# mLSTM passes of a two-block kernel: a fourth query buffer, another bank for the turn, another order of the squares, and the query scaling on VectorE

## What is computed

```
m_t   = maximum(b + m, max(dmat))
a     = exp(b + m - m_t)
qk    = einsum(q, k) * exp(dmat - m_t)
num   = a * einsum(q, C) + einsum(qk, v)
den   = a * einsum(q, n) + sum(qk)
h     = num / maximum(abs(den), exp(-m_t))
h_lat = hl_f + flip(hl_b)
y     = sigmoid(o) * rms_norm(h, g) * silu(z)
```

## Time and profile before

| | us |
|---|---|
| median of 3 runs (lowest, highest) | 3209.8 (3208.81, 3211.93) |
| the profiled execution's own time | 3207.7 |
| its span, first to last instruction | 3206.0 |
| TensorE matmul busy in the span | 3024.7 (94%) |
| VectorE busy | 1479.2 (46%) |
| ScalarE busy | 1156.3 (36%) |
| GpSimd busy | 146.7 (5%) |
| mlstm stage of layer 0, from its first score to its last post | 79.2 |
| mlstm stage of layer 1 | 53.9 |

### The profile page before, as it was taken

One profiled execution on the slowest core, in us unless ns is written; L12 is line 12 of the kernel. 1 busy time (PEld: TensorE's weight loads), 2 busy tenths in 40 slices (PEclk: granted clock), 3 DMA queues, 4 the chain that ended last, 5 costly groups with the idle time before them and its releaser, 6 DMA issues.

```text
span 3206.0 us, 38631 instructions
## 1 busy us (share of the span) xinstructions
PE 3024.7 (94%) x15614; PEld 2460.2 (77%) x15614; DVE 1479.2 (46%) x1970; ACT 1156.3 (36%) x1822; POOL 146.7 (5%) x206
## 2 busy tenths in 40 slices
PE   7999999999999999988999699999999899889988
PEld 5777888777788877867888588868877688768666
DVE  4645445544555555383432522153445644432344
ACT  4334233434443343163241521162222534331342
POOL 1000000000000000000000300100000000300100
PEclk9999999999999999999999799999999999989999
DMA  4243232330422221101112311312111022221322
GB/s 172 93 152 110 105 118 88 122 130 27 145 92 95 102 79 58 55 7 61 41 60 76 69 66 47 105 30 72 53 61 58 23 79 86 79 85 53 113 69 79
DMA packets 44710, 257.76 MB, mean 80 GB/s; under 512 B 6344, under 2 KB 6352, under 8 KB 20768
## 3 DMA queue, kind: packets, MB, share of 16 engines
q1 hardware_dynamic: 30528, 204.30, 17.9%
q0 software_dynamic: 14048, 51.56, 5.1%
HBM read 251.56 MB, written 4.28 MB: 80 GB/s over the span
## 4 chain that ended last, share of the span: by engine, by line
PE 85%; DVE 7%; ACT 3%; DMA 2%; issue 2%; POOL 1%; SPq 0%; DVEq 0%; ACTq 0%; POOLq 0%
PE PS L732 14%; PE PS L733 14%; PE PS L734 14%; PE PS L713 7%; PE PS L712 7%; PE PS L714 7%; PE PS L678 2%; PE PS L676 2%; PE PS L677 2%; DVE SMALL L2307 1%; PE PS L913 1%; PE PS L1007 1%; PE PS L1023 1%; PE PS L997 1%; PE PS L992 1%
## 5 line engine op out<-in xcount | busy, mean ns | idle before, releaser
L732 PE MATMUL PS<-HHX,WHX 128*128 128x512 f32 (+1 forms) x1600 | 567.4, 355 | 40.3 <-DVE WLM L2157 31.3
L733 PE MATMUL PS<-HL,WHX 128*128 128x512 f32 (+1 forms) x1600 | 567.7, 355 | 0.0
L1481 ACT ACTIVATE WHX<-W 128x2048 fp32r<-128x2048 f32 x108 | 186.1, 1723 | 611.2 <-DMA W<-in_w 389.5
L732 PEld LDWEIGHTS PS<-HHX,WHX 128*128 128x128 f32 x1600 | 308.2, 193 | 85.7 <-issue 33.2
L734 PE MATMUL PS<-HHX,WLX 128*128 128x512 f32 (+1 forms) x1024 | 355.9, 348 | 0.0
L733 PEld LDWEIGHTS PS<-HL,WHX 128*128 128x128 f32 x1600 | 306.9, 192 | 41.6
L2157 DVE TENSOR_TENSOR WLX<-W,WHX 128x2048 fp32r<-128x2048 f32 x60 | 137.5, 2292 | 381.1 <-ACT WHX L1481 381.0
L713 PE MATMUL PS<-HL,WH 128*128 128x512 f32 x672 | 265.4, 395 | 0.0
L712 PE MATMUL PS<-HH,WH 128*128 128x512 f32 x672 | 263.3, 392 | 0.0
L714 PE MATMUL PS<-HH,WL 128*128 128x512 f32 x672 | 261.7, 389 | 0.0
L2157 DVE TENSOR_TENSOR WL<-W,WH 128x2048 fp32r<-128x2048 f32 x68 | 155.9, 2292 | 221.6 <-ACT WH L1481 221.6
(11 more groups left out here) (500 smaller groups left out, 5711.3 us busy)
## 6 DMA issues: line engine op xcount, KB each, us to landing
W<-in_w SPq DMA_DIRECT2D x172, 1024.0 KB, 4.7
XC<-in_wm POOLq DMA_DIRECT2D x12, 1024.0 KB, 5.1
H<-in_wm POOLq DMA_DIRECT2D x12, 1024.0 KB, 5.7
W<-in_wb SPq DMA_DIRECT2D x24, 512.0 KB, 3.2
W<-in_w SPq DMA_DIRECT2D x8, 768.0 KB, 4.1
ARENA<-mrow POOLq DMA_DIRECT2D x18, 256.0 KB, 4.9
PR<-in_nbias POOLq DMA_DIRECT2D x12, 256.0 KB, 2.9
ARENA<-in_nbias POOLq DMA_DIRECT2D x12, 256.0 KB, 2.9
```

Source lines behind the costliest of these rows:

```text
L732: pe.matmul(dst, wh[:, s, c], hi[:, k, t0:t1], start=k == 0, stop=False)
L733: pe.matmul(dst, wh[:, s, c], lo[:, k, t0:t1], start=False, stop=False)
L1481: act.activation(dst[:, s, 0:n], W[:, s, 0:n], ACT.Copy).then_inc(wh_ready[s], 1)
```

## The change

Six edits, all in the mlstm stage.

1. QS has four buffers, not three; the fourth takes the place that CS0 had, and all eight states CS lie in the enlarged SELP. The fetch of query weights for pass p+4 stands beside the fetch of decays for p+4.
2. The query multiplication leaves GpSimd (`pool_queries` is gone) and is done by VectorE (`dve_queries`): for pass 0 ahead of everything in the stage, for pass p+1 behind `probs` of p+1 and ahead of `dens` of p.
3. The turn of head u writes to bank (u + 1) % 2, a bank of scores. It waits no longer for divide_forward; the forward outputs wait no longer for ml_y; the scores of pair u (u of 3 or more) wait for ml_y of pair u-3.
4. ScalarE takes the squares of the head before ahead of divide_forward, not behind it.
5. The context's decay rows are fetched once (256 values), not twice, and the mask's addition writes the second copy that a masked block needs.
6. ml_u0 and ml_u1 are one semaphore, ml_u, counted to the same places.

```
-    DM, QS = [RST[:, 0:T], DM1, DM2, DM3], [PR[:, 0:T], QS1, QS2]
-    CS = [CS0] + [SELP[:, k * (P + 1):(k + 1) * (P + 1)] for k in range(7)]
+    DM, QS = [RST[:, 0:T], DM1, DM2, DM3], [PR[:, 0:T], QS1, QS2, QS3]
+    CS = [SELP[:, k * (P + 1):(k + 1) * (P + 1)] for k in range(8)]
...
                 pe.wait_ge(sem("ml_zm"), past("ml_zm", ly) + 2 * (u - 1))
+            if u >= 3:
+                pe.wait_ge(sem("ml_y"), past("ml_y", ly) + u - 2)
...
-            if d == 0 and u >= 2:
-                pe.wait_ge(sem("ml_y"), past("ml_y", ly) + u - 1)
...
             pe.wait_ge(sem("ml_scaled"), past("ml_scaled", ly) + u + 1)
-            pe.wait_ge(sem("ml_divf"), past("ml_divf", ly) + min(u + 2, np_ // 2))
...
-                mm = pe.transpose(PS[:, 2, i * P:(i + 1) * P], HB[:, h, T * g + i * P:T * g + (i + 1) * P], IDENT[:, :])
+                mm = pe.transpose(PS[:, (u + 1) % 2, i * P:(i + 1) * P], HB[:, h, T * g + i * P:T * g + (i + 1) * P], IDENT[:, :])
...
             if it["d"] == 0:
-                divide_forward(it)
                 if it["u"]:
                     squares(passes[p - 1])
+                divide_forward(it)
...
+    def dve_queries(dve, st, it):
+
+        ly, l, h = st.layer, it["l"], it["h"]
+        if it["g"]:
+            return
+        done = 16 * state_uses[l % 4] if ly else 0
+        dve.wait_ge(sem(f"ml_bw{l % 4}"), done + 16 * (l // 4 + 1))
+        dve.tensor_tensor(QS[l % 4], QS[l % 4], Q[:, h, 0:T], ALU.mult).then_inc(sem("ml_qs"), 1)
...
+        dve_queries(dve, st, passes[0])
         states(passes[0])
         probs(passes[0])
...
                 probs(passes[p + 1])
+                dve_queries(dve, st, passes[p + 1])
             dens(it)
...
-            src = mrow[ly, row, T:TA].unsqueeze(0).broadcast_to([2, TC]).partition_broadcast(P)
-            dst = DM[p % 4].rearrange("p (a b) -> p a b", a=2)
+            src, dst = mrow[ly, row, T:TA].partition_broadcast(P), DM[p % 4][:, it["d"] * TC:(it["d"] + 1) * TC]
...
                 pool_mask(pool, st, passes[p + 2])
-                pool_queries(pool, st, passes[p + 2])
             if p + 4 < np_:
                 pool_decay_rows(pool, st, passes[p + 4])
-            if p + 3 < np_:
-                pool_query_rows(pool, st, passes[p + 3])
+                pool_query_rows(pool, st, passes[p + 4])
```

More of the change, by code:

```diff
@@ L436, in build @@
     cv = Carve(scratch)
-    DM1, DM2, DM3, QS1, QS2 = (cv(T) for _ in range(5))
-    KTX, CS0 = cv(8, P), cv(P + 1)
+    DM1, DM2, DM3, QS1, QS2, QS3 = (cv(T) for _ in range(6))
+    KTX = cv(8, P)
     assert cv.at <= hyb_at + 2 * KT * SLAB
-    DM, QS = [RST[:, 0:T], DM1, DM2, DM3], [PR[:, 0:T], QS1, QS2]
-    CS = [CS0] + [SELP[:, k * (P + 1):(k + 1) * (P + 1)] for k in range(7)]
+    DM, QS = [RST[:, 0:T], DM1, DM2, DM3], [PR[:, 0:T], QS1, QS2, QS3]
+    CS = [SELP[:, k * (P + 1):(k + 1) * (P + 1)] for k in range(8)]
     HB = K
@@ L452, in build @@
     slot_uses = [len(range(k, n_ml, 4)) for k in range(4)]
-    state_uses = [len(range(k, n_lat, 3)) for k in range(3)]
+    state_uses = [len(range(k, n_lat, 4)) for k in range(4)]
     in_layer0 = dict(
         da_probs=n_da, da_evac=n_da, da_o=n_da, da_max=n_da, da_half=16, da_scaled=8, da_turned=8, da_rs=8, da_y=8,
-        ml_s=n_mu, ml_u0=n_lat, ml_u1=n_lat, ml_c0=n_lat, ml_c=3 * n_lat, ml_masked=n_ml, ml_qs=n_lat, decay=n_ml,
+        ml_s=n_mu, ml_u=2 * n_lat, ml_c0=n_lat, ml_c=3 * n_lat, ml_masked=n_ml, ml_qs=n_lat, decay=n_ml,
         ml_zm=n_ml, ml_o=n_ml, ml_dens=n_mu, ml_divf=n_mu, ml_divb=n_mu, ml_rs=n_mu, ml_scaled=n_mu,
@@ L460, in build @@
         rope_done=8, na_probs=2 * n_na, na_max=n_na, na_values=n_na, v_stored=16 * 8, v_blocks=16 * 7,
-        **{f"ml_bm{k}": 16 * slot_uses[k] for k in range(4)}, **{f"ml_bw{k}": 16 * state_uses[k] for k in range(3)})
+        **{f"ml_bm{k}": 16 * slot_uses[k] for k in range(4)}, **{f"ml_bw{k}": 16 * state_uses[k] for k in range(4)})
     def past(name, layer):
@@ L1148, in states @@
             s0, s1, s2, _ = later_blocks(d)
-            for b, done, groups in ((6, "ml_u0", ((4, 5), (s0,))), (7, "ml_u1", ((s1,), (s2,)))):
+            for b, groups in ((6, ((4, 5), (s0,))), (7, ((s1,), (s2,)))):
                 if l:
@@ L1158, in states @@
                                        skip_group_check=True)
-                mm.then_inc(sem(done), 1)
+                mm.then_inc(sem("ml_u"), 1)
         def ahead(it):
@@ L1188, in outs @@
                     mm = pe.matmul(PS[:, pair + j // 2, (P + 1) * (j % 2):(P + 1) * (j % 2 + 1)],
-                                   QS[l % 3][:, j * P:(j + 1) * P], CS[(4 * l + n) % 8], start=False, stop=True,
+                                   QS[l % 4][:, j * P:(j + 1) * P], CS[(4 * l + n) % 8], start=False, stop=True,
                                    skip_group_check=True)
@@ L2701, in pool_query_rows @@
             return
-        if l >= 3:
-            old = [e["p"] for e in st.passes if e["g"] == 0][l - 3]
+        if l >= 4:
+            old = [e["p"] for e in st.passes if e["g"] == 0][l - 4]
             pool.wait_ge(sem("ml_o"), past("ml_o", ly) + old + 1)
-        pool.dma_start(QS[l % 3], wrow[ly, row, :].partition_broadcast(P)).then_inc(sem(f"ml_bw{l % 3}"), 16)
+        pool.dma_start(QS[l % 4], wrow[ly, row, :].partition_broadcast(P)).then_inc(sem(f"ml_bw{l % 4}"), 16)
     def pool_mask(pool, st, it):
@@ L2712, in pool_mask @@
         v = DM[p % 4].rearrange("p (a b) -> p a b", b=P)
+        src = v
         if it["g"]:
-            v = v[:, 0:4:3, :]
-        n = v.shape[1]
-        mask = (MFWD, MBWD)[d].unsqueeze(1).broadcast_to([P, n, P])
-        pool.tensor_tensor(v, v, mask, ALU.add).then_inc(sem("ml_masked"), 1)
-    def pool_queries(pool, st, it):
-        ly, l, h = st.layer, it["l"], it["h"]
-        if it["g"]:
-            return
-        done = 16 * state_uses[l % 3] if ly else 0
-        pool.wait_ge(sem(f"ml_bw{l % 3}"), done + 16 * (l // 3 + 1))
-        pool.tensor_tensor(QS[l % 3], QS[l % 3], Q[:, h, 0:T], ALU.mult).then_inc(sem("ml_qs"), 1)
+            src, v = v[:, 2 * d:2 * d + 2, :], v[:, 0:4:3, :]
+        mask = (MFWD, MBWD)[d].unsqueeze(1).broadcast_to([P, v.shape[1], P])
+        pool.tensor_tensor(v, src, mask, ALU.add).then_inc(sem("ml_masked"), 1)
     def pool_mlstm(pool, st):
@@ L2735, in pool_mlstm @@
             pool_decay_rows(pool, st, passes[p])
-            if p < 3:
-                pool_query_rows(pool, st, passes[p])
+            pool_query_rows(pool, st, passes[p])
         pool_mask(pool, st, passes[1])
-        pool_queries(pool, st, passes[1])
         for it in passes:
@@ L2843, in _ @@
                 pool_mask(pool, next_st, next_st.passes[0])
-                pool_queries(pool, next_st, next_st.passes[0])
             if st.kind == "mlstm":
```

10 lines of the change are left out of this document (5 added, 5 removed).

## The result

| | before | changed |
|---|---|---|
| device time, median | 3209.3 us (4 runs, 3208.0 to 3211.9) | 3183.1 us (4 runs, 3181.8 to 3184.7) |
| ratio | | 0.9918, 95% interval 0.9900 to 0.9935 |
| profiled execution: own time, span | 3207.7, 3206.0 us | 3184.2, 3182.3 us |
| layer 0 stage, first score to last post | 79.2 us | 62.2 us |
| layer 1 stage | 53.9 us | 44.8 us |

The change saves 26.2 us, 0.8% of the kernel. In the profiled executions the two stages got shorter by 17.0 and 9.1 us, 26.1 together, while the spans differ by 23.7: the changed execution came into the stage of layer 0 2.6 us later (first scores at 1758.40 against 1755.79), and the delay is older than the parts that the change touches, since GpSimd's store of the decay rows ahead of them stands at 1602.89 against 1600.33 already. Between and behind the stages the two executions agree within 0.3 us.

The account below looks back on a forecast made before the run. It held the mlstm stages bound by engines waiting on each other; 15.9 us less in layer 0 and 8.8 in layer 1 made 3207.7 into 3183.0, and the median's 2.1 on top gave 3185 us, range 3174 to 3199.

Parts of the forecast that it names:

- a circle of waits over root, scale, turn and post: Both mlstm stages: engines wait on each other in a loop, none full; cutting it saves 24.7 us together.
- The sum by stages: Pair and end times summed per mlstm stage: layer 0 15.9 us less, layer 1 8.8, together 24.7.
- the context's 5.3 a pair: Layer 0's three context pairs: 5.3 us each instead of 7.1, bounds 3.9 and 7.1, 5.4 us less.
- The one ahead of the stage puts 0.6 us on the path: Start of each stage: VectorE's query multiplication for the first pass adds 0.6 us.
- VectorE and TensorE are nearly equal, they hand work to each other, so 9.0: Latent pairs: VectorE 7.7 + 0.7 us, TensorE 8.1; a pair taken at 9.0, bounds 8.1 and 10.1.
- The port, 0.7 us a pair: Latent pairs: VectorE operations meeting GpSimd masks lose up to 0.73 us each, 0.7 a pair, bounds 0 and 2.2.
- Rival A: Latent pairs: each query multiplication and scale meets a GpSimd mask, pairs take 10.1 us; 3195 us, chance 0.17.
- Squares first: ScalarE: squares and root, 2.2 us, fill time waiting for denominators; the root comes one division earlier.
- Rival C: ScalarE: squares ahead delay each division up to 2.2 us and give the gain back; 3206 us, chance 0.09.
- GpSimd is off the path: Latent pairs: GpSimd keeps 4.7 us of work a pair, and query weights fetched four passes ahead cost VectorE no wait.
- Turn bank: TensorE: two waits go, and scores wait for the post of pair u-3, about 1 us, within TensorE's slack.
- Rival D: Latent pairs: TensorE stays at its lower clock level, 15.4 us a pair; 3231 us, chance 0.05.

Follow-up runs that it names:

- A2: The changed kernel with the squares behind the division again; ratio 1.0001 to the kernel before, stages 77.9 and 53.5 us.
- F2: The changed kernel with every query multiplication issued twice on VectorE; ratio 0.9951 to the kernel before, stages 65.4 and 50.5 us.
- F1: The changed kernel with VectorE's query multiplication ahead of the states of the same pass; ratio 0.9901 to the kernel before, stages 58.7 and 43.6 us.
- G1: The changed kernel with ScalarE's copy of the next first state ahead of the division; ratio 0.9909 to the kernel before, stages 58.5 and 42.4 us.
- A4: The changed kernel with three query buffers and the fetch three passes ahead; ratio 0.9930 to the kernel before, stages 61.0 and 44.8 us.
- A1: The changed kernel with the query multiplications back on GpSimd; ratio 0.9911 to the kernel before, stages 58.5 and 41.8 us.
- A3: The changed kernel with the turn in bank 2 and its old waits again; ratio 0.9951 to the kernel before, stages 66.9 and 48.3 us.
- E3: The kernel before with only the squares moved ahead of the division; ratio 0.9960 to the kernel before, stages 71.0 and 48.2 us.
- E1: The kernel before with the fourth query buffer, GpSimd still multiplying; ratio 0.9982 to the kernel before, stages 76.1 and 50.2 us.

## Why the prediction was right

3185 us was forecast, with 3174 to 3199 around it, and 3183.1 came. The cause named, a circle of waits over root, scale, turn and post that the edits cut, is what the waits and A2 show. That single terms met their lengths to 0.3 us is luck in part, as said below. By its steps:

- **The sum by stages.** Layer 0 was to lose 15.9 us and lost 17.0; layer 1 8.8 and lost 9.1. A latent pair was put at 9.0 and took 8.95; the fourth 7.2, took 6.87; three context pairs 16.0, took 15.74; the ends 8.0 and 13.0, took 8.2 and 13.4 (1820.63 - 1812.42, 2796.90 - 2783.50). Two of these hits are luck. The average of 11.1 us hid that the first pair took only 7.72 before: it became longer, not shorter, and the three behind it gained 5.5, 3.5 and 2.9. And the context's 5.3 a pair met a profile in which TensorE's clock fell there; at a clock of 1.00 the same passes took 13.9 to 14.5 us for three, 4.6 to 4.8 a pair.
- **"The one ahead of the stage puts 0.6 us on the path": wrong.** From first score to first forward outputs it is 4.53 us after and 4.50 before. The first multiplication is there, 0.68 us at 1760.56, but the outputs are no later for it: before, VectorE had short waits there, 0.38 us for TensorE's updates and some 0.2 ahead of the first state.
- **"VectorE and TensorE are nearly equal, they hand work to each other, so 9.0": right in size, not in cause.** VectorE is busy 7.8 and 7.9 us in the second and third pair, the time at the port included, where 7.7 + 0.7 was counted; but it is the bound by itself there (F2), and what comes on top is one definite wait of 0.8 us behind ScalarE's division (F1 and G1 take it away), not a general loss in handing over. The 9.0 was a choice between bounds, and in the first pair another chain, over the first states, gave the same length.
- **The port, 0.7 us a pair: near on the mean, wrong in its bound.** The four disturbed multiplications of layer 0 took 1.45, 0.97, 1.29 and 0.97 for 0.68: 2.0 us over four pairs, 0.5 each, and scale met no mask. Rival A, each time, did not come; but 0.73 us is not the most that one can lose, see below.
- **Squares first: right, and undersold.** It was listed as one of six edits that fill idle time; it is the one without which nothing is left (A2). Rival C, that this order gives back the gain, was the wrong way round.
- **The fourth buffer and "GpSimd is off the path": true in the settled pairs, and the buffer is worth 0.7 us at most by the profile** where the queries are on VectorE (A4). The prediction did not see that moving the queries costs time once the buffer is there: 2.5 and 2.3 us in the latent pairs (A1).
- **Turn bank: the new wait was expected at about 1 us in each pair, and is 1.2 us once** in the latent passes of layer 0 and 0.8 to 1.4 us four times at the context's scores; what the removed waits are worth, 8.2 us (A3), had no term of its own.
- **Rival D** did not come: the clock rose to 0.92 and 0.97 as the idle stretch went, and was 1.00 over the latent pairs.

## What to carry to other kernels

When several engines work lists in order, look for a result that an engine needs at once and that another engine makes only behind a step which itself waits for the first engine. Here one swap of two calls on ScalarE decided 24 us, as much as the whole change, while moving work to another engine cost time. And after such a cut count the list of the fullest engine in one period and name each gap in it: the one that was left here, 0.8 us a pair, could be closed by moving one line (F1: 2.3 us in the latent pairs of each layer, 5.0 us by the medians). Compare like with like when you read such a gain: a part of the program that the edit does not touch can run at another clock.

## What the runs showed of the hardware

VectorE's multiplication of 128x512, 0.68 us alone, when it is held up by GpSimd's mask, ends a fixed time after the mask's end, wherever in the mask it begins, and in some cases also when by its record it began a little before it:

| kernel | VectorE from, us | GpSimd's mask | VectorE to | behind the mask's end |
|---|---|---|---|---|
| changed | 1766.79 | 1766.39 to 1767.68 | 1768.24 | 0.56 |
| changed | 1775.89 | 1775.34 to 1776.63 | 1777.18 | 0.55 |
| G1 | 1775.58 | 1775.60 to 1776.88 | 1777.44 | 0.56 |
| F2 | 1765.25 | 1765.34 to 1766.61 | 1767.17 | 0.56 |
| A3 (scale) | 1786.16 | 1786.51 to 1787.80 | 1788.36 | 0.56 |

The rows of the first and the last line, VectorE's and then GpSimd's:

```profile
1766.79 1.45 DVE L2527 TENSOR_TENSOR ARENA<-ARENA 128x512 f32<-128x512 f32 x1
```

```profile
1766.39 1.29 POOL L2726 TENSOR_TENSOR ARENA<-ARENA,MASKS 128x512 f32<-128x512 f32 x1
```

```profile
1786.16 2.20 DVE L2600 TENSOR_TENSOR ARENA<-ARENA,SMALL 128x512 f32<-128x512 f32 x1
```

```profile
1786.51 1.29 POOL L2727 TENSOR_TENSOR ARENA<-ARENA,MASKS 128x512 f32<-128x512 f32 x1
```

In the profiles of all kernels here, 75 meetings in which VectorE took over 0.70 us end 0.54 to 0.57 us behind GpSimd's instruction. So a meeting costs VectorE from 0 to 1.7 us (2.37 in E3 against 0.69), and the more the earlier in the mask it comes; GpSimd then pays 0.01 or 0.02 us. Two meetings, both in E1, are longer: a scale that began at 1775.19 beside a multiplication of GpSimd's that ended at 1775.45 took 1.90 us and ended 0.59 behind the two fetches issued after it.

The other outcome exists too. Here VectorE began 0.38 us ahead, kept its 0.68 us, and GpSimd's mask took 1.44 us for 1.27 (F1, layer 1):

```profile
2769.66 0.68 DVE L2527 TENSOR_TENSOR ARENA<-ARENA 128x512 f32<-128x512 f32 x1
```

```profile
2770.04 1.44 POOL L2726 TENSOR_TENSOR ARENA<-ARENA,MASKS 128x512 f32<-128x512 f32 x1 [1.64 <-DMA ARENA<-mrow]
```

The Trainium skill's page "SBUF — State Buffer", section "Who interferes with whom", says that the order of issue decides who blocks. The first two lines of the table and the rows of F1 agree; the last three lines, in which VectorE's record starts 0.02, 0.09 and 0.35 us ahead of the mask's and VectorE still loses, do not, unless a record starts earlier than the instruction takes the port, which no run here can show. By the same page a VectorE instruction with at most one input in SBUF, outside the modes in which it uses both of its ports, does not contend with GpSimd, and the probabilities of the changed kernel bear that out, undisturbed beside the mask of 1775.34 to 1776.63:

```profile
1775.29 0.68 DVE L2544 SCALAR_TENSOR_TENSOR ARENA<-PS,ARENA 128x512 f32<-128x512 f32 x1
```
